# Fused two-block network on one core: last gate chunk by column blocks, hybrid block started on the unnormalised residual

## The reference, cut to what matters

```python
def rmsnorm_2(x, g):
    xf = x.astype(F32)
    y = xf * lax.rsqrt(jnp.mean(xf * xf, axis=-1, keepdims=True) + NORM_EPS)
    return (y * g.astype(F32)).astype(x.dtype)

def first_block(x, ...):
    ...
    return rmsnorm(h, final_norm_g)

def second_block(x, p, ...):
    h = x
    for i in range(DEPTH):
        j = i // 2
        hn = rmsnorm_2(h, attn_norm[i])
        if i % 2 == 0:
            mix = sb_rwkv_mixer(hn, hyb_w_in[j], ...)
        else:
            mix = mla_mixer(hn, positions, mla_w_down[j], ...)
        h = h + mix
        h = h + conv_glu(rmsnorm_2(h, ffn_norm[i]), ...)
        e = rmsnorm_2(p[i] @ ple_w_proj[i], ple_norm[i])
        gate = jax.nn.sigmoid(rmsnorm_2(h, ple_gate_norm[i]) @ ple_w_gate[i])
        h = h + gate * e
    return rmsnorm_2(h, final_norm)
```

## Time and profile before

| | before |
|---|---|
| median of 3 runs | 1323.04 us (1322.97 to 1324.91) |
| profiled execution | 1323.27 us |
| its span | 1321.5 us, 1.77 us less |
| TensorE matmul busy | 1300.0 us, 98% |
| TensorE weight loads busy | 1268.0 us, 96% |
| DVE busy | 913.0 us, 69% |
| ACT busy | 758.1 us, 57% |
| POOL busy | 44.1 us, 3% |
| share of the last chain on TensorE | 87% |

### The profile page before, as it was taken

How to read it: one execution, slowest core, us unless ns; L and a number is a source line. 1 busy time by engine, 2 the same in 40 slices (tenths; PEclk the granted TensorE clock), 3 DMA queues, 4 the chain that set the end, 5 groups by cost and what they waited for, 6 DMA issues and landing times.

```text
span 1321.5 us, 29315 instructions
## 1 busy us (share of the span) xinstructions
PE 1300.0 (98%) x12222; PEld 1268.0 (96%) x12222; DVE 913.0 (69%) x1297; ACT 758.1 (57%) x977; POOL 44.1 (3%) x37
## 2 busy tenths in 40 slices
PE   9999999999999999999999999999999999999997
PEld 8999999998899999999989899999999889999997
DVE  4789886488479876468746387666578779666556
ACT  6667665367657665357554166554476876554444
POOL 1010000010010000010000010000001001000000
PEclk9999999999999999999999999999999999999999
DMA  8455555545345555535401135555435335555520
GB/s 333 175 208 191 191 190 191 191 191 195 125 160 191 191 190 191 191 122 191 160 34 37 65 136 211 182 184 199 179 141 187 130 128 200 192 190 190 191 96 33
DMA packets 31981, 220.63 MB, mean 167 GB/s; under 512 B 3712, under 2 KB 3840, under 8 KB 6160
## 3 DMA queue, kind: packets, MB, share of 16 engines
q1 hardware_dynamic: 30672, 213.36, 44.7%
q0 software_dynamic: 784, 4.85, 1.1%
q10 hardware_dynamic: 432, 1.05, 0.2%
HBM read 218.20 MB, written 1.05 MB: 166 GB/s over the span
## 4 chain that ended last, share of the span: by engine, by line
PE 87%; DVE 8%; ACT 3%; issue 1%; DMA 1%; POOL 0%; SPq 0%; DVEq 0%; ACTq 0%; POOLq 0%
PE ps L1850 22%; PE ps L1851 21%; PE ps L1852 21%; PE ps L1861 17%; DVE w_lo L1102 2%; PE ps L1856 2%; PE ps L1857 2%; PE ps L1858 2%; ACT w_hi L503 1%; DVE xt L1154 1%; PE ps L2072 1%; DMA raw<-stream 1%; DVE xA L1164 1%; DVE xB L1164 0%; DVE xB L1126 0%
## 5 line engine op out<-in xcount | busy, mean ns | idle before, releaser
L1102 DVE TENSOR_TENSOR w_lo<-raw,w_hi 128x2048 fp32r<-128x2048 f32 x197 | 449.9, 2288 | 149.3 <-ACT w_hi L503 148.8
L503 ACT ACTIVATE w_hi<-raw 128x2048 fp32r<-128x2048 f32 x197 | 376.2, 1913 | 169.8 <-PE ps L1852 165.4
L1850 PE MATMUL ps<-xB,w_hi 128*128 128x256 f32 x1120 | 314.4, 281 | 1.7 <-DVE up_acc L1228 1.7
L1852 PE MATMUL ps<-xB,w_lo 128*128 128x256 f32 x1120 | 312.7, 279 | 0.0
L1851 PE MATMUL ps<-xB,w_hi 128*128 128x256 f32 x1120 | 312.6, 279 | 0.0
L1850 PEld LDWEIGHTS ps<-xB,w_hi 128*128 128x128 f32 x1120 | 210.5, 188 | 3.1 <-DVE up_acc L1228 1.9
L1850 PE MATMUL ps<-xA,w_hi 128*128 128x256 f32 x744 | 210.7, 283 | 0.5 <-DVE w_lo L1102 0.5
L1851 PEld LDWEIGHTS ps<-xB,w_hi 128*128 128x128 f32 x1120 | 210.5, 188 | 0.1
L1852 PEld LDWEIGHTS ps<-xB,w_lo 128*128 128x128 f32 x1120 | 210.5, 188 | 0.0
L1851 PE MATMUL ps<-xA,w_hi 128*128 128x256 f32 x744 | 207.7, 279 | 0.0
L1852 PE MATMUL ps<-xA,w_lo 128*128 128x256 f32 x744 | 207.6, 279 | 0.0
(11 more groups left out here) (295 smaller groups left out, 1909.3 us busy)
## 6 DMA issues: line engine op xcount, KB each, us to landing
raw<-stream SPq DMA_DIRECT2D x199, 1024.0 KB, 4.8
raw<-stream SPq DMA_DIRECT2D x4, 512.0 KB, 7.6
at_bias<-rel POOLq DMA_DIRECT2D x1, 2048.0 KB, 8.1
hT<-x_t SPq DMA_DIRECT2D x4, 256.0 KB, 7.0
lora_w<-lora POOLq DMA_DIRECT2D x1, 1024.0 KB, 5.1
out_t<-xt SPq DMA_DIRECT2D x4, 256.0 KB, 2.4
hcon<-hyc POOLq DMA_DIRECT2D x1, 576.0 KB, 4.0
wsT<-wst ACTq DMA_DIRECT2D x1, 512.0 KB, 4.4
```

The costliest lines, as they stand in the source:

```text
L503: nc.scalar.activation(w_hi[c.slot][:], raw[c.slot][:], ACT.Copy).then_inc(hi_made, 1)
L1102: nc.vector.tensor_tensor(w_lo[c.slot][:], raw[c.slot][:], w_hi[c.slot][:].bitcast(F32), ALU.subtract).then_inc(lo_made, 1)
L1850: nc.tensor.matmul(out, wh, xh, start=start, stop=False, skip_group_check=True)
L1852: return nc.tensor.matmul(out, wl, xh, start=False, stop=stop, skip_group_check=True)
```

## The change

Between the blocks: the norm N_FIN1 is gone from the list of norms. With h the residual before it, r1 the root of its mean square and g1, g2 the two weights, the hybrid block's input is h g1 g2 r1 r2, where r2 is the root for h g1 r1. `hy_gain` holds g1 g2 and is made ahead of ffn 1. The early operands for N_HY are h times `hy_gain`, made at each quarter's update inside `ffn(1)`. ACT squares h (for r1) and h g1 (for the mean square of h g1, in two `slot` tiles); POOL takes no part, DVE adds both sets. `sum_folded` makes four sums. ACT makes r1 (`fin_rs`), DVE the mean square times r1 squared, ACT r2, DVE r1 r2. The `split_hi` of chunk 4 moves ahead of `round_x`, its `split_lo` ahead of `scale_early`. The new residual h g1 r1 is made by eight DVE products during the matrix products.

At the end: the last gate chunk is computed one column block after the other, into halves of two banks; the sigmoid, the product, the addition and the square of a block follow each half (`last_gate`, `gate_tail`). The sums of blocks 0 and 2 stand inside the second half, those of the last two k behind it with eight filler products between. hT times the last weight is made ahead of the root (`gained`), and four products of 128x512 with the root replace the eight of 128x256.

```diff
...
 OUT_GATED, OUT_FF0, OUT_KV, OUT_Q, OUT_FF1, OUT_HY, OUT_FF2, OUT_PL0, OUT_FF3, OUT_PL1 = range(10)
-N_GM, N_FF0, N_AT, N_FF1, N_FIN1, N_HY, N_FF2, N_PL0, N_ML, N_FF3, N_PL1, N_FIN2 = range(12)
+N_GM, N_FF0, N_AT, N_FF1, N_HY, N_FF2, N_PL0, N_ML, N_FF3, N_PL1, N_FIN2 = range(11)
...
 SCALED_AT = {n: sum(c for m, (_, c) in EARLY.items() if m < n) for n in EARLY}
-FOLDED = tuple(n for n in range(12) if n not in (N_FIN1, N_FIN2))
-ADDED_BY = {n: sum(2 if m in FOLDED else 1 for m in range(n)) for n in range(12)}
+FOLDED = tuple(range(N_FIN2))
+POOLED = {n: 0 if n == N_HY else 2 if n in FOLDED else 1 for n in range(11)}
+ADDED_BY = {n: sum(POOLED[m] for m in range(n)) for n in range(11)}
 FOLD_AT = {n: i for i, n in enumerate(FOLDED)}
 FINAL_XT = 8 * 10
-FILL = (3, 9)
 GATE_BANK = (4, 6, 7, 5)
...
             return (2 * i + b) % 3 if i < BESIDE else 2 * ((i + 2) % 4) + b
+        def early_gain(n, k):
+
+            return hy_gain[:, k:k + 1] if n == N_HY else col(EARLY[n][0], k)
+
         def early_tile(n):
...
             for b in range(4):
-                sp.wait_ge(xt_made, FINAL_XT + 2 * b + 2)
+                sp.wait_ge(xt_made, FINAL_XT + b + 1)
                 sp.dma_start(out[:, 2 * b:2 * b + 2], xt[:, 2 * b:2 * b + 2]).then_inc(stored, 16)
...
             add_squares(N_FF1)
-            add_squares(N_FIN1)
             pool.wait_ge(h_updated, 16)
...
             pool.dma_start(w0b, bass.AP(w0.tensor, 0, [[0, P], [1, 512]])).then_inc(hy_landed, 16)
-            add_squares(N_HY)
             pool.wait_ge(x_lo_made, 5 * (OUT_HY + 1))
...
                     last = nc.scalar.activation(early_tile(n)[:, k, 0, :], hT[:, k, :], ACT.Copy,
-                                                scale=col(EARLY[n][0], k))
+                                                scale=early_gain(n, k))
                 last.then_inc(raw_hi, 1)
...
             ffn(1, N_FF1)
-            square_norm(N_FIN1)
             c0 = C0["hy"]
...
                 square(N_HY, b)
+                for k in (2 * b, 2 * b + 1):
+                    last = nc.scalar.activation(slot[2 + k // 4][:, k % 4, :], hT[:, k, :], ACT.Square, scale=col("fin1", k))
+                last.then_inc(fin_sq, 1)
             split_hi(Chunk(c0).ahead())
-            root_norm(N_HY)
+            act.wait_ge(ss_summed, N_HY + 1)
+            inverse_root(fin_rs[:], half(4, 0), D, fin_made)
+            act.wait_ge(fin_mean, 1)
+            inverse_root(rs[:], rs[:], 1, rs_made)
+            split_hi(Chunk(c0 + 1).ahead())
             round_x(OUT_HY, xA)
...
             act.wait_ge(mu_ready, 1)
-            split_hi(Chunk(c0 + 1).ahead())
             hy_copy(0)
...
                         split_hi(c.ahead())
+                    elif i:
+                        square(n + 1, 2, preload=False)
+                        act.wait_ge(gate_half, 1)
+                        nc.scalar.activation(pl_sg[1][:, 0, :], half(5, 0), ACT.Sigmoid).then_inc(g_on, 1)
+                        act.wait_ge(chunk_used, c.count(1))
+                        nc.scalar.activation(pl_sg[1][:, 1, :], half(1, 0), ACT.Sigmoid).then_inc(g_on, 1)
+                        nc.scalar.preload_act_table_set("natural_log_exp_and_others")
+                        break
                     act.wait_ge(chunk_used, c.count(1))
                     if g >= 2:
-                        act.wait_ge(h_updated, 4 * (n if i == 0 else n) + g - 1)
+                        act.wait_ge(h_updated, 4 * n + g - 1)
                     nc.scalar.activation(pl_sg[g % 2][:], ps[:, GATE_BANK[g], :].rearrange("p (b t) -> p b t", b=2),
...
                 for k in range(KD):
-                    nc.vector.scalar_tensor_tensor(out=xt[:, k, :], in0=hT[:, k, :], scalar=col(gain, k), in1=rs[:],
+                    nc.vector.scalar_tensor_tensor(out=xt[:, k, :], in0=hT[:, k, :],
+                                                   scalar=early_gain(N_HY, k) if o == OUT_HY else col(gain, k), in1=rs[:],
                                                    op0=ALU.mult, op1=ALU.mult).then_inc(xt_made, 1)
...
                     last = nc.vector.scalar_tensor_tensor(out=early_tile(n)[:, k, 1, :], in0=hT[:, k, :],
-                                                          scalar=col(EARLY[n][0], k),
+                                                          scalar=early_gain(n, k),
                                                           in1=early_tile(n)[:, k, 0, :].bitcast(F32), op0=ALU.mult,
...
                     rest_early(n + 1, 3)
-                if n + 1 in FOLDED:
+                if n + 1 in FOLDED and n + 1 != N_HY:
                     fold_squares(n + 1)
+                if n + 1 == N_HY:
+                    for b in (0, 4):
+                        dve.wait_ge(sq_made, 4 * N_HY + b // 2 + 2)
+                        own.mark(nc.vector.tensor_tensor(xt[:, b + 2:b + 4, :], xt[:, b + 2:b + 4, :], xt[:, b:b + 2, :],
+                                                         ALU.add))
+                    own.wait()
+                    nc.vector.tensor_tensor(xt[:, 6:8, :], xt[:, 6:8, :], xt[:, 2:4, :], ALU.add).then_inc(sq_folded, 1)
+                    dve.wait_ge(fin_sq, 4)
+                    for i in (2, 3):
+                        own.mark(nc.vector.tensor_tensor(slot[i][:, 0:2, :], slot[i][:, 0:2, :], slot[i][:, 2:4, :], ALU.add))
+                    own.wait()
+                    nc.vector.tensor_tensor(slot[2][:, 0:2, :], slot[2][:, 0:2, :], slot[3][:, 0:2, :],
+                                            ALU.add).then_inc(fin_folded, 1)
                 split_lo(Chunk(d0 + PAIRS - 1).ahead())
...
             scale_x(OUT_FF1, xA, "f_norm1")
+            link(nc.vector.tensor_tensor(hy_gain[:, 0:KD], col("fin1", 0, KD), col("at_norm0", 0, KD), ALU.mult))
             ffn(1, N_FF1)
-            root(N_FIN1)
-            for k in range(KD):
-                ins = nc.vector.scalar_tensor_tensor(out=hT[:, k, :], in0=hT[:, k, :], scalar=col("fin1", k), in1=rs[:],
-                                                     op0=ALU.mult, op1=ALU.mult)
-                if k % 2:
-                    ins.then_inc(h_updated, 1)
-
+            c0 = C0["hy"]
+            dve.wait_ge(fin_made, 1)
+            link(nc.vector.scalar_tensor_tensor(out=rs[:], in0=half(4, 1), scalar=1.0 / D, in1=fin_rs[:], op0=ALU.mult,
+                                                op1=ALU.mult))
+            nc.vector.tensor_tensor(rs[:], rs[:], fin_rs[:], ALU.mult).then_inc(fin_mean, 1)
+            split_lo(Chunk(c0).ahead())
             nc.vector.tensor_scalar(om_mu[:], col("rw_mu", 0, 15), -1.0, 1.0, ALU.mult, ALU.add).then_inc(mu_ready, 1)
-            dve.wait_ge(h_updated, 20)
-            for b in range(4):
-                rest_early(N_HY, b)
-            fold_squares(N_HY)
-            c0 = C0["hy"]
-            split_lo(Chunk(c0).ahead())
             root(N_HY)
+            link(nc.vector.tensor_tensor(rs[:], rs[:], fin_rs[:], ALU.mult))
             scale_x(OUT_HY, xA, "at_norm0")
+            split_lo(Chunk(c0 + 1).ahead())
             def diagonal(tile):
...
             scale_early(N_HY, 2, c0 + 2, 2)
-            split_lo(Chunk(c0 + 1).ahead())
             shift(2)
...
             split_lo(Chunk(c0 + 12).ahead())
+            for k in range(KD):
+                nc.vector.scalar_tensor_tensor(out=hT[:, k, :], in0=hT[:, k, :], scalar=col("fin1", k), in1=fin_rs[:],
+                                               op0=ALU.mult, op1=ALU.mult).then_inc(fin_scaled, 1)
             with_eye(14, 7, -1)
...
                 dve.wait_ge(chunk_used, co + g + 1)
+                if g == 0:
+                    dve.wait_ge(fin_scaled, KD)
                 add_quarter(g, 4 + g)
...
             ffn(2, N_FF2)
+
+            def gained(k):
+                own.mark(nc.vector.tensor_scalar(pl_sq[:, k, :], hT[:, k, :], col("fin2", k), None, ALU.mult))
+
+            def gate_tail(n):
+
+                for b in range(2):
+                    dve.wait_ge(g_on, 8 + b)
+                    link(nc.vector.tensor_tensor(pl_sg[1][:, b, :], pl_sg[1][:, b, :], pl_e[:, 6 + b, :], ALU.mult))
+                    link(nc.vector.tensor_tensor(hT[:, 6 + b, :], hT[:, 6 + b, :], pl_sg[1][:, b, :], ALU.add))
+                    nc.vector.tensor_tensor(xt[:, 6 + b, :], hT[:, 6 + b, :], hT[:, 6 + b, :], ALU.mult).then_inc(tail_sq, 1)
+                    gained(6 + b)
             def ple(i):
...
                         split_lo(c.ahead())
+                    if i and g == 3:
+                        gate_tail(n)
+                        break
                     dve.wait_ge(g_on, 4 * i + g + 1)
...
                         split_lo(Chunk(c0 + 3).ahead())
+                    if i and g:
+                        dve.wait_ge(h_updated, 4 * n + g + 1)
+                        for k in (range(4), (4, 5))[g - 1]:
+                            gained(k)
                     if n + 1 in EARLY and g:
...
             ple(1)
+            own.wait()
```

(56 more changed lines are left out.)

5 lines of the change are left out of this document (3 added, 2 removed).

## The result

The changed kernel takes 1330.43 us (median of 11 runs, 1326.68 to 1331.91) against 1324.09 of the kernel before (11 runs, 1322.97 to 1327.55): a ratio of 1.0040, with a 95% interval of 1.0028 to 1.0051. The forecast was 1315.8, faster.

A forecast was written before the change was run, and what follows sets the result against it. TensorE, busy 98%, was taken as the bound, with stalls at the hybrid block's start and the end. Gains of 5.8 + 1.4 = 7.2 us from 1323.27 gave 1316.1, as median 1315.8; range 1313.9 to 1318.3.

The forecast's parts named there:

- Units: Durations read from the old trace for all steps: 0.1167 us a matmul, 5.6 us a chunk, 0.43 us a sum.
- step 6: Matrix products: eight DVE products for the true residual (3.25 us) are covered with 0.65 us to spare; hy_gain costs nothing.
- the one for "slower": Rival, 4%: from 593 to the matrix products the hybrid block loses its granted clock repeatedly; 25 us of it gives 1328.
- the wait for fin_folded: Hybrid block's first pair of chunks: TensorE waits 0.9 us for the folded squares of the last two sums.
- before chunk 4: Hybrid block's start: TensorE waits 1.5 us for bank 0, as the moved w_lo delays scale_early and the copy.
- before the lora products: Behind chunk 4: TensorE stands 2.4 us, from 600.5 to 602.9, for the shift of group 3.
- D to L: From DVE's first add at the end of ffn 1 to the first lora product; forecast gain 5.8 us.
- the eight products covered: Matrix products: DVE's residual products fit its idle time, 0.65 us to spare; rival that they do not, 6%, up to 3.25 lost.
- the longer switch: The end: by the skill's 2.66 us per table switch the last root starts some 0.3 us later, gain 1.1.
- The 44.46: Profiled us of the kernel before for D to L, from which the forecast counted its 5.8 us gain.
- The clock rival: 28%: the clock falls behind the new gaps at the hybrid block's start; after the third it costs 1.7 us, 1317.5.
- a new wait of over 1 us in the matrix products: Sign that the forecast is wrong: no further wait was expected up to the matrix products.

The follow-up runs named there:

- after: The changed kernel as first measured and profiled, against the kernel before: 1330.43 us, ratio 1.0040.
- a_high: The changed kernel with hy_gain allocated behind all other tiles of its stage, so old tiles keep their places: 1320.75 us, ratio 0.9979 to the kernel before.
- a_again: The changed kernel measured once more, no edit: 1329.48 us, ratio 1.0046 to the kernel before.
- tail_only: The kernel before with only the change's end part put in: 1320.92 us, ratio 0.9988.
- fetch_10: order_fill with ten more 64x64 products (40 instructions) after the warm-up: 1314.96 us, ratio 0.9944 to the kernel before.
- a_256: The changed kernel with hy_gain 256 bytes long instead of 128, half unused: 1320.18 us, ratio 0.9976 to the kernel before.
- best: order_fill with twenty more 64x64 products (80 instructions) after the warm-up, timed again in six runs: 1315.86 us, ratio 0.9940 to the kernel before.
- order_fill: The changed kernel with 256-byte hy_gain, chunk 4's w_lo behind scale_early on DVE, and ten filler records before chunk 4: 1315.93 us, ratio 0.9942 to the kernel before.

## Why the prediction was wrong

**The failing step** is "Units": one matmul at 0.1167 us for the whole kernel, and with it the last words of step 6, "hy_gain is one small operation ahead of ffn 1 ...: nothing". I costed the tile's operation, not its 128 bytes. They shift the place of the moving operands of all dense matmuls, from 116.7 ns each to 117.3 in ffns 1 and 3 and 118.7 in ffns 0 and 2: after and a_high differ in that alone and by 9.7 us of median (a_again by 8.7 on the same chip). No rival held it; the one for "slower" was a clock that stays low, and the clock was 0.996 over the kernel, 0.997 before.

**Confirmed by after's rows**, each counted from D: the pair starts at once (4.03 us, forecast 4.00); the wait for fin_folded 0.49 (0.9); before chunk 4 1.10 (1.5); before the lora products 2.23 (2.4); D to L 6.03 shorter (5.8); the eight products covered with 0.49 to spare (0.65). The end: the four sums without a wait, sixteen filler records in 1.78 us (1.86), 1.4 us gained in the profile of tail_only (1.4). The table load held nothing up: it ended at 1322.52, and the Ln started when its sum came, at 1323.48; with the longer switch that the prediction set beside its sum it would have started at 1323.90.

**Wrong in size.** The 44.46 taken as the kernel's own had a low-clock stretch in it: 1.5 of the 5.8. I had read it and counted its loss among the gains, though it hangs on one execution.

**The clock rival** (28%) came true: 1.8 us forecast at 1.7, behind the third wait, and filler took it away. My witness against it, a single 2.03 with the clock kept, was a matter of the execution too: the low level follows this wait in nine of the nineteen profiles, here in fetch_10:

```profile
67.00:68.00 1.00, 1.00 (x6) 1.00 (x6) 1.00 (x2) 0.00 (x0) 0.00 (x0) 0.50 0.00 0
68.00:69.00 1.00, 1.00 (x7) 1.00 (x6) 1.00 (x1) 0.66 (x1) 0.00 (x0) 0.50 0.46 66
```

**Not foreseen:** "a new wait of over 1 us in the matrix products" was named as a sign of error and came, 2.03 us, but from the instruction queue, which no step of the prediction had in it. The sum of the parts is 7.2 - 1.5 - 1.8 - 0.3 = 3.6, against 3.3 and 3.4 measured for a_256 and a_high.

## To carry to other kernels

Before a new tile is put among old ones, look at what it moves: on this kernel 128 bytes cost 8.7 to 11 us, and rounding the tile up to 256, or putting it last, cost nothing. If a kernel gets slower everywhere, count matmuls in equal windows of stages that were not edited, before you look at the edit. And a gain read from one execution is to be compared with a second: here one low-clock stretch was a fifth of the forecast gain.

## What the runs showed of the hardware

- The distance of 128x256 matmuls goes with the place of the moving operand within 256 bytes: 116.7 ns at the old place and 256 bytes further, 117.8 at 32, 117.3 to 120.0 at 128, at a granted clock of 1.00. At one place it can take another value after a pause (xB in ffn 2 of after, 117.3 ahead of the wait and 118.7 behind it; in best 116.7 and 117.8).
- TensorE's instructions come in packets of 16 KB, which the trace lists among those of the DMA engines that load the weights (72 in after), and a packet due during a 1 MB load came 1 to 3 us late (703.5 in fetch_10, 708.0 in order_fill); TensorE then stood for up to 2.06 us, or not at all. The Trainium skill's page "Runtime: NRT & Kernel Launch" (section "Instruction fetch mechanics") gives 16 KiB blocks of 256 instructions, fetched ahead and mostly hidden. The size agrees with the trace, and so do the products, two instructions each and 3.95 us for 128. That it is hidden does not hold in these 64x64 products, some 30 ns each.
- The same waits are followed by the low clock in one execution and not in another: 1.32 and 0.72 in two of eight profiles, the single 2.03 in nine of nineteen. The 2.2 us behind waits of 0.5 and 1.1 was followed by it in all four.
